# Stick-breaking attention over the prompt: the causal mask of the last key block, as a VectorE addition in the odds' tile or as TensorE products with the identity

## The reference, cut to what matters

```
def stick_breaking_block(q, q_pos, k, v, k_pos, sb_bias):
    z = jnp.einsum('bqhd,blhd->bhql', q, k).astype(jnp.float32) * (HEAD_DIM ** -0.5)
    z = z + sb_bias.astype(jnp.float32)[None, :, None, None]
    mask = (k_pos[None, :] < q_pos[:, None])[None, None]
    log_1m = jnp.where(mask, jax.nn.log_sigmoid(-z), 0.0)
    suffix = lax.cumsum(log_1m, axis=3, reverse=True) - log_1m
    a = jnp.where(mask, jnp.exp(jax.nn.log_sigmoid(z) + suffix), 0.0)
    o = jnp.einsum('bhql,blhd->bqhd', a.astype(v.dtype), v)
```

## Time and profile before

| | |
|---|---|
| median of 3 runs | 1999.79 us (1998.95 to 2004.87) |
| profiled execution | 2009.53 us, of which span 2007.7 us |
| mean granted TensorE clock | 0.966 |
| busy over the whole span | PE 1872.1 us, PEld 1604.4, DVE 997.6, ACT 588.0, POOL 117.0 |
| the stage of the change | about 646 to 771 us of the span |

### The profile page before, as it was taken

One profiled execution on the slowest core, in us unless ns is written; L12 is line 12 of the kernel. 1 busy time (PEld: TensorE's weight loads), 2 busy tenths in 40 slices (PEclk: granted clock), 3 DMA queues, 4 the chain that ended last, 5 costly groups with the idle time before them and its releaser, 6 DMA issues. The chain is left out here.

```text
span 2007.7 us, 30752 instructions
## 1 busy us (share of the span) xinstructions
PE 1872.1 (93%) x11646; PEld 1604.4 (80%) x11646; DVE 997.6 (50%) x1992; ACT 588.0 (29%) x982; POOL 117.0 (6%) x209
## 2 busy tenths in 40 slices
PE   7999999999777788899968999999999999999996
PEld 5777779999445555666658889999999999999995
DVE  5202442000264786565648274556546545555647
ACT  4211001121583575333322043122122122212113
POOL 0000000000100302323100001000000000000000
PEclk9999999999788789999969999999999999999998
DMA  6444447511611927999936315021112112102102
GB/s 221 170 170 170 175 170 279 204 45 56 173 29 47 326 91 277 372 385 390 347 136 225 103 43 173 22 63 42 34 50 63 31 31 63 42 21 63 42 15 109
DMA packets 138581, 274.40 MB, mean 137 GB/s; under 512 B 23641, under 2 KB 76522, under 8 KB 135978
## 3 DMA queue, kind: packets, MB, share of 16 engines
q1 hardware_dynamic: 116586, 154.59, 23.2%
q0 software_dynamic: 21888, 118.38, 16.1%
HBM read 243.24 MB, written 78.97 MB: 160 GB/s over the span
## 5 line engine op out<-in xcount | busy, mean ns | idle before, releaser
L2164 DVE TENSOR_TENSOR tl_x<-tl_x,tl_ps 128x512 f32<-128x512 f32 (+1 forms) x198 | 135.1, 686 | 188.4 <-PE tl_ps L2394 185.4
L499 PE MATMUL tl_ps<-tl_T_lo,tl_up_hi 128*128 128x364 f32 (+1 forms) x1008 | 222.4, 329 | 0.0
L499 PE MATMUL tl_ps<-tl_T_hi,tl_up_lo 128*128 128x364 f32 (+1 forms) x1008 | 222.4, 329 | 0.0
L499 PE MATMUL tl_ps<-tl_T_hi,tl_up_hi 128*128 128x364 f32 (+1 forms) x1008 | 222.3, 329 | 0.0
L499 PEld LDWEIGHTS tl_ps<-tl_T_hi,tl_up_hi 128*128 128x128 f32 x1008 | 175.0, 188 | 0.9
L499 PEld LDWEIGHTS tl_ps<-tl_T_hi,tl_up_lo 128*128 128x128 f32 x1008 | 174.8, 188 | 0.0
L499 PEld LDWEIGHTS tl_ps<-tl_T_lo,tl_up_hi 128*128 128x128 f32 x1008 | 174.8, 188 | 0.0
L469 PE MATMUL fr_ps<-fr_w_hi,h_hi 128*128 128x512 f32 x384 | 154.2, 401 | 2.7 <-DVE h_lo L365 2.7
L469 PE MATMUL fr_ps<-fr_w_lo,h_hi 128*128 128x512 f32 x384 | 152.6, 397 | 0.0
L469 PE MATMUL fr_ps<-fr_w_hi,h_lo 128*128 128x512 f32 x384 | 152.6, 397 | 0.0
L2394 PE MATMUL tl_ps<-tl_dn_hi,tl_f_hi 128*128 128x512 f32 x360 | 141.0, 392 | 0.0
(11 more groups left out here) (318 smaller groups left out, 3428.0 us busy)
## 6 DMA issues: line engine op xcount, KB each, us to landing
out_s<-in_cache POOLq DMA_DIRECT2D x8, 4080.0 KB, 20.3
all_lead<-in_w_up SPq DMA_DIRECT2D x44, 512.0 KB, 4.7
fr_raw<-in_w_in POOLq DMA_DIRECT2D x9, 2048.0 KB, 8.9
pg_pages<-in_pool POOLq DMA_DIRECT2D x64, 256.0 KB, 6.4
pg_pages<-in_pool SPq DMA_DIRECT2D x64, 256.0 KB, 7.6
pg_odds<-in_pool SPq DMA_DIRECT2D x64, 256.0 KB, 7.8
zs<-fr_zt SPq DMA_DIRECT2D x48, 256.0 KB, 2.0
tl_dn_raw<-in_w_down SPq DMA_DIRECT2D x22, 512.0 KB, 4.5
```

Of the source, the lines that this page charges most:

```text
L499: last = pe.matmul(out[:, n * 512:n * 512 + b - a], lhs, rhs[:, a:b], start=(i == 0), stop=(i == len(pairs) - 1))
L2164: dve.tensor_tensor(x, x, banks[m % len(banks)][0:n, :], ALU.add).then_inc(added, 1)
```

## The change

The two mask products per pair are gone, and with them the last stop of the accumulation: the scores' products now start and stop by themselves. Instead VectorE, in `exponents`, waits until its own copies of the pair are complete and then adds the 128 by 128 constant `strict` to the last block of each head's tile in `odds`, in place, two additions per pair, 32 in all. `take_odds` on ScalarE waits for the new semaphore `masked` in place of `z_done`. The constant is transposed, since the product with the identity transposed it before.

```
--- before.py
+++ after.py
@@ -97,7 +97,7 @@
         c0 = 3 * P + 4 * NS + NS * g
         dec[:, c0:c0 + NS] = np.where((delta >= 0) & (delta % dil == 0) & (group[:, None] == 0), 0.0, dec[:, c0:c0 + NS])
     later = (a[:, None] >= a[None, :]).astype(np.float32)
-    strict = np.where(a[:, None] < a[None, :], 0.0, BIG).astype(np.float32)
+    strict = np.where(a[:, None] > a[None, :], 0.0, BIG).astype(np.float32)
     strict01 = (a[:, None] < a[None, :]).astype(np.float32)
     b, j = np.arange(SROWS)[:, None] // NS, np.arange(SROWS)[:, None] % NS
     col = np.arange(NB * 4 * NS)[None, :]
@@ -874,6 +874,7 @@
             "z_ready", "z_done", "odds_done", "soft_done", "scanned", "left_done", "a_done"))
         own_in, zeroed, padded, chain_a, chain_d, c_done, spread_done = (s.sem(n) for n in (
             "own_in", "zeroed", "padded", "chain_a", "chain_d", "c_done", "spread_done"))
+        masked = s.sem("masked")
         page_turned, page_moved = s.sem("page_turned"), [s.sem("act_page_moved"), s.sem("dve_page_moved")]
         ORDER = (0, 1, 4, 6, 7, 5, 3, 2)
         TURN_NEW, SCORE_NEW, SUM_NEW = 2, 4, 6
@@ -976,7 +977,7 @@
 
             def take_odds(n):
                 L = length(n // 2)
-                act.wait_ge(z_done, 2 * wave_after(n // 2) + n % 2 - 1)
+                act.wait_ge(masked, n + 1)
                 act.activation(odds[:, n % 8, 0:L], odds[:, n % 8, 0:L], ACT.Exp, scale=SCALE).then_inc(odds_done, 1)
 
             def soften(n):
@@ -1097,6 +1098,11 @@
                         dve.tensor_scalar(odds[:, (2 * p + h) % 8, c], zbank[:, bank:bank + c.stop - c.start],
                                           bias_z[:, 2 * hp + h:2 * hp + h + 1], Z_MAX / SCALE, ALU.add,
                                           ALU.min).then_inc(z_done, 1)
+                L = length(p)
+                dve.wait_ge(z_done, 2 * wave_after(p))
+                for h in range(2):
+                    x = odds[:, (2 * p + h) % 8, L - P:L]
+                    dve.tensor_tensor(x, x, K["strict"][:, :], ALU.add).then_inc(masked, 1)
 
             def scan(n):
                 L = length(n // 2)
@@ -1161,17 +1167,12 @@
                 pe.wait_ge(moved, t_at["rows", qt] + 1)
                 for w in range(waves[p]):
                     i, c = w_at[p] + w, wave_cols(p, w)
-                    diagonal = w == waves[p] - 1
                     if i >= 2:
                         pe.wait_ge(z_done, 2 * (i - 1))
                     for h in range(2):
                         part, bank = slice(h * HD, h * HD + HD), (i % 2 * 2 + h) * 512
                         last = pe.matmul(zbank[:, bank:bank + c.stop - c.start], qk[part, qt, hp, :],
-                                         qk[part, c.start // P:c.stop // P, 2 + hp, :], start=True, stop=not diagonal)
-                    if diagonal:
-                        for h in range(2):
-                            end = (i % 2 * 2 + h) * 512 + c.stop - c.start
-                            last = pe.matmul(zbank[:, end - P:end], K["strict"][:, :], K["ident"][:, :], start=False, stop=True)
+                                         qk[part, c.start // P:c.stop // P, 2 + hp, :], start=True, stop=True)
                     last.then_inc(z_ready, 1)
 
             def turn_new():
```

## The result

The changed kernel takes 2006.01 us (median of 16 runs, 2000.90 to 2010.33), the kernel before 1999.47 (16 runs, 1990.47 to 2004.87). The ratio is 1.0033 with an interval of 1.0022 to 1.0043: slower by 4.4 to 8.6 us, where no change was forecast.

A forecast was written before the change was run, and what follows sets the result against it. The prediction took the loop as bound by VectorE in some passes, by TensorE and ScalarE in turn in the others. Gains and costs per pair summed to -0.3 us: 1999.79 - 0.3 = 1999.5 us, range 1995 to 2006.

The forecast's parts named there:

- The start: Pairs 0 to 2 gain up to 3 us, lost at `pad_new`, which waits through TensorE for a DMA: shift 0.
- Pairs 2 to 5: Waits swallow two uncovered masks of 0.52 us each; TensorE's queue is a little earlier: VectorE -0.1 us at 689.7.
- the ledger: Running count, pass by pass, of how many us VectorE is earlier (-) or later (+) than in the kernel before.
- Pairs 6 to 15: Pairs 6, 7, 9, 11 gain at waits before scans, most others lose 0.4 to 0.52 us: -0.75 becomes about -0.3.
- The end: Pair 15 costs nothing, having no more score copies behind it; page loads do not hold the stage's end: about -0.3 us.
- The additions: 32 VectorE additions, 0.41 us plus 0.11 of wait, so 0.52 us a pair; 8.3 us for 16 pairs if uncovered.
- rival 1: VectorE sets every pass, between copies and next scan: each mask costs its full 0.52 us, at most 8.3; chance 0.15.
- Rival 2: Less TensorE work lowers the clock; five passes after pair 8 lose 1.4 us each, 7 us, 2006.8 us; chance 0.07.
- The sign I had named: Wrong if the changed stage is over 4 us longer: VectorE has no gaps left, or the clock is well below 0.83.
- Rival 3: All masks covered, the products' time comes through at ScalarE-released scan starts and early pairs: -4.7 us, 1995.1 us; chance 0.16.
- The sum: All passes of the changed stage together: -0.3 us, later stages shifted as a whole, giving 1999.5 us; chance 0.62.

The follow-up runs named there:

- x5: The changed kernel plus two unread TensorE products per pair, placed in TensorE's idle time, for all pairs; ratio to the kernel before 1.0004.
- x12: The same kernel as x5 run again, on another chip; ratio to the kernel before 1.0027.
- x13: x5 plus 12 unread products while TensorE waits for the samples' rows early in the stage; ratio to the kernel before 1.0015.
- x4: The kernel before without any mask, neither products nor additions, so outputs are not the reference's; ratio to the kernel before 1.0005.
- x6: The kernel before with the mask products replaced by a mask tile in VectorE's existing clip, no additions; ratio to the kernel before 0.9998.
- x9: The changed kernel plus two unread TensorE products per pair in idle time, only for pairs 0 to 5; ratio to the kernel before 1.0000.
- x10: The changed kernel plus two unread TensorE products per pair in idle time, only for pairs 10 to 15; ratio to the kernel before 1.0015.
- x3: The changed kernel with its VectorE additions and TensorE's mask products kept as well; ratio to the kernel before 1.0024.
- x8: x6 plus two unread TensorE products per pair in idle time, for all pairs; ratio to the kernel before 1.0005.
- x11: x8 plus 12 unread products while TensorE waits for the samples' rows early in the stage; ratio to the kernel before 0.9997.
- x15: The changed kernel without further edit, run a third time; ratio to the kernel before 1.0036.
- x2: The changed kernel without further edit, run again; ratio to the kernel before 1.0051.
- x7: The changed kernel with every VectorE addition made twice, 64 in all; ratio to the kernel before 1.0039.
- x14: The kernel before plus 12 unread products while TensorE waits for the samples' rows early in the stage; ratio to the kernel before 1.0012.

## Why the prediction was wrong, step by step

**The start.** Right within 0.7 us: the gain of the first pairs is lost at `pad_new`, which waits for a DMA. What I did not ask is what TensorE does meanwhile. Its wait there grew from 0.67 us to 3.2, and the mask's four records per pair were gone too. The low clock, in which the stage begins anyway, lasted until 27.2 us instead of 19.5; with records put back in other places it lasted until 15.6 and 16.7 (x5, x12), and with that wait filled as well until 9.3 (x13).

**Pairs 2 to 5: the step that failed.** I took "-0.1 at 689.7" with TensorE's durations read off the trace of before. They hold only at the clock of before: the scores of pair 4 took 2.50 us instead of 1.35. By the scan of pair 6 the change is 3.2 us later (51.7 against 48.5 us, means of three and two profiles) where the ledger had 0.75 earlier. x4 and x6 show most of this lag (51.2) without any addition, x5, x12 and x9 do not show it (47.6 to 48.9) with all additions: 2.7 of the 3.2 us are the clock, and some 0.5 the additions.

**Pairs 6 to 15.** Right in size: the ledger let VectorE lose 0.4 us net over them (-0.75 to about -0.3), measured is a gain of 0.4 (68.0 against 68.3 and 68.4 us). Masks under waits and products' time handed back do nearly cancel there; the gap before pair 9's scan closed, those before 7 and 11 shrank by 1.3 and 1.5 us, that before 6 by 0.1, where I had half a microsecond for each. The sizes of both terms can be read off x4: the products' time handed back is 2.8 us and the additions take 2.4.

**The end.** I counted nothing after pair 15. Measured is 1.6 us (8.3 against 6.8), at the transposes of pages that fell into a low stretch. Of this x10 won back 0.7. It is not the missing products that put them there: x3, with the products kept, has the low transposes (3.07 us) and an end of 8.2 us too, while x4 and x6, with neither, have 6.8. There the low stretch lies some 4 us earlier, ahead of the transposes.

**The additions.** 0.49 us a pair with 0.03 of wait before it, 0.52 forecast. Like with like, they lengthen the stage by 1.3 us where the products stay (x3 against before) and by 1.0 to 2.0 where products stand in idle time (x5 and x12 against x8, x13 against x11), but by 4.4 where there are no products (the change against x4 and x6). So rival 1's full 8.3 us are nowhere, and about half of its price is there in the change: the other half fell on waits.

**The rivals.** Rival 2, the clock, is what happened together with a part of rival 1, and it got a chance of 0.07. That its price, 2006.8 us, comes so near the measured 2006.01 is luck: I placed it in the passes after pair 8, at 1.4 us each, and there the clock did not fall. The windows of that stretch, after and then before:

```profile
690.40:745.00 54.60, 40.12 (x298) 24.11 (x296) 51.23 (x63) 43.02 (x61) 0.00 (x0) 0.87 0.42 141
```

```profile
694.00:746.00 52.00, 40.68 (x280) 25.05 (x279) 44.68 (x45) 40.02 (x57) 0.00 (x0) 0.84 0.44 148
```

It is 0.87 after and 0.84 before; the clock struck at the start, where TensorE waits for a DMA, and at the end. The sign I had named, a stage longer by over 4 us with a clock well below 0.83, did come: 4.4 us and 0.77. Against the clock I had held that the products that remain are the greater part. The rule named beside it, from the Trainium skill's TensorE: Matmul & The Clock Gate, Part 1, that activity releases the throttle, agrees with x5 (0.85 against 0.77 for the change) and x11 (0.86 against x6's 0.78), where products that nobody reads raise the clock. Rival 3, the products' time coming through, is excluded by x4, where it should have come through most: 1.0005 (0.9990 to 1.0021), and 4.7 us less would be 0.9977.

**The sum.** 3.2 - 0.4 + 1.6 = 4.4 us for the stage, against -0.3. It lies at the lower edge of the measured 4.4 to 8.6 us. By x3 and x4 the same 4.4 us are 1.3 for the additions alone, 0.0 for the missing products alone, and 3.1 that only the two together bring; the rows of one kernel, from which the ledger took all its durations, show none of these 3.1.

**What stays open.** The ratios of the change, 1.0033, 1.0036 and 1.0051, are 6.6 to 10 us, more than the stage's 4.4, and x12 and x13 are some 5 and 3 us above before with stages that are not longer by more than 1.1. Outside the stage no profile shows a lasting difference: the samples' stage is 259.8 and 258.5 us before, 257.6, 259.7 and 257.5 with the change, the tail 975.5 and 976.3 against 975.4, 975.4 and 975.1. The clocks of the timed executions say where most of it is: 5.3 and 6.6 of the 7.0 and 8.6 us of x15 and x2 go with a lower clock, which was thus lower over all executions and not only in the profiled ones. In x12 and x13 the clock is that of before, and their 3 us belong to the additions and the unread products together. Why x3's additions cost 3.6 us of time at one clock and only 1.3 of stage in its profile is open, and so is how much of the clock's part lies in this stage in the timed executions.

## What to carry to other kernels

Durations of TensorE read from a trace are durations at that trace's clock: before work is taken off TensorE in a stage that already runs partly at the lower level, look at the granted clock by windows and ask where TensorE will idle instead, above all ahead of a DMA that does not move. And do not add up the two halves of a move, work taken off one engine and put on another, from rows of a single kernel: here they came to 1.3 and 0.0 us one by one and to 4.4 together. The saved time can come back as a longer low stretch, at another place than the edit. And where an elementwise pass with a free operand is there already, put the mask into it before it is weighed which engine should carry it: the fused copy cost nothing on either, and x6 is some 4 us of stage below the change, though no faster than before.

## What the runs showed of the hardware

- TensorE products that nobody reads shortened a stage: 32 of them (64 records) took the changed kernel's from 128.0 us to 123.7 and 124.7 (x5, x12), and 12 more (24 records) to 123.1 (x13). In the kernels with the fused mask the steps were from 123.7 to 122.7 and 121.6 (x6, x8, x11), one profile each, where two profiles of one kernel differed by 1.3.
- The same eight records of fp32 score products took 2.50 us in a stretch with a granted clock of 0.50 and 1.35 in one with 1.00; 16 fp32 transposes of 128x128 took 3.12 and 1.91 us.
- The same instructions of the dilated stage took 124.1 us with 32 us at the lower clock and 131.7 with 53 (x2, x4), wider than the 4.4 us of the changed stage. The two do not go strictly together: x7's took 124.4 us with 25, and x14's 128.5 with 50.
- Over the timed executions of one kernel a mean granted clock higher by 0.001 went with 1.0 us less of some 2000.
- A clip against a tile (scalar_tensor_tensor, PSUM and SBUF in) took 0.743 us for 128x512, a clip against a number 0.742 to 0.743 from PSUM.
- An fp32 addition of 128x128 in SBUF took 0.288 us; one that waited for the instruction ahead on its own engine started 0.03 us behind it.
